# The high part of each weight slab copied in two halves, the first as soon as TensorE is half through the slab two back

## What is computed

```python
def first_block(x, meta_tokens, ...):
    h = rmsnorm(h_res, norm_g[l])
    proj = h @ w_in[l]
    glu_a, glu_b, z_conv, q, f, i, g_rec, m_conv, m_rec = jnp.split(proj, split_idx, axis=-1)
    y_conv = conformer_branch(glu_a, glu_b, z_conv, ...)     # gated conv of width 31, layernorm, silu, @ w_out
    y_rec = hgrn2_branch(q, f, i, g_rec, ...)                # 8 heads, decaying linear recurrence
    merged = jax.nn.sigmoid(m_conv) * y_conv + jax.nn.sigmoid(m_rec) * y_rec
    h_res = h_res + merged @ w_out[l]
def second_block(x, ...):
    n = rms_norm(x, mix_norm_g[l]); proj = jnp.einsum('bsd,de->bse', n, w_in[l])
    mixed = jnp.concatenate([y_a, y_b, y_c], axis=-1)        # chunked attention, short conv, spatial gating
    x = x + jnp.einsum('bse,ed->bsd', mixed, w_out[l])
    hdn = jnp.square(jax.nn.relu(jnp.einsum('bsd,df->bsf', rms_norm(x, mlp_norm_g[l]), w_up[l])))
    x = x + jnp.einsum('bsf,fd->bsd', hdn, w_down[l])
# third block: mLSTM of 4 heads with gates from the projection, pooling over windows of
# 2, 4, 8 and 16 tokens, output projection, layer norm, MLP of 4096, layer norm
```

## Time and profile before

| | us |
|---|---|
| median of 3 runs | 3816.53 |
| lowest and highest | 3816.52, 3818.11 |
| profiled execution, its time | 3818.15 |
| profiled execution, its span | 3816.8 |
| TensorE busy | 3702.0 (97%) |
| VectorE busy | 1701.3 (45%) |
| ScalarE busy | 1177.3 (31%) |
| GpSimd busy | 1095.4 (29%) |
| mean granted clock of TensorE, share of full | 0.986 |

### The profile page before, as it was taken

How to read it: one execution, slowest core, us unless ns; L and a number is a source line. 1 busy time by engine, 2 the same in 40 slices (tenths; PEclk the granted TensorE clock), 3 DMA queues, 4 the chain that set the end, 5 groups by cost and what they waited for, 6 DMA issues and landing times.

```text
span 3816.8 us, 42159 instructions
## 1 busy us (share of the span) xinstructions
PE 3702.0 (97%) x17644; PEld 3027.0 (79%) x17644; DVE 1701.3 (45%) x2132; ACT 1177.3 (31%) x1523; POOL 1095.4 (29%) x747
## 2 busy tenths in 40 slices
PE   6999999999999999999999999999999999999998
PEld 6888887888878876777788888887777878888886
DVE  5655624999652473224442222225657652222226
ACT  4554532222241243444321211114323241111113
POOL 3334321222233451111442222224212442222223
PEclk9999999999999999999999999999999999999999
DMA  2000011111232240001221111113111321111112
GB/s 102 28 29 28 28 62 60 56 56 53 69 133 92 97 151 34 33 33 34 100 73 49 45 50 45 50 45 120 49 33 34 105 71 46 50 44 45 50 45 77
DMA packets 64988, 229.29 MB, mean 60 GB/s; under 512 B 7200, under 2 KB 7328, under 8 KB 64672
## 3 DMA queue, kind: packets, MB, share of 16 engines
q1 hardware_dynamic: 64800, 226.60, 18.0%
HBM read 201.40 MB, written 25.17 MB: 59 GB/s over the span
## 4 chain that ended last, share of the span: by engine, by line
PE 88%; DVE 7%; issue 2%; ACT 2%; POOL 1%; DMA 1%; SPq 0%; DVEq 0%; ACTq 0%
PE psum L505 76%; PE psum L617 2%; PE psum L853 2%; PE psum L868 2%; PE psum L883 1%; DVE Ab L2130 1%; PE psum L588 0%; DVE qb L2176 0%; PE psum L702 0%; PE psum L739 0%; POOL wl L3115 0%; PE psum L641 0%; PE psum L640 0%; DVE fb L2095 0%; DVE fb L2087 0%
## 5 line engine op out<-in xcount | busy, mean ns | idle before, releaser
L3115 POOL TENSOR_TENSOR wl<-raw,wh 128x512 fp32r<-128x512 f32 x636 | 889.7, 1419 | 2380.1 <-ACT wh L1185 2380.1
L505 PE MATMUL psum<-hh,wh 128*128 128x512 f32 (+2 forms) x3760 | 1188.4, 392 | 38.2 <-POOL wl L3115 15.7
L505 PE MATMUL psum<-hh,wl 128*128 128x512 f32 (+2 forms) x3760 | 1149.8, 381 | 0.0
L505 PE MATMUL psum<-hl,wh 128*128 128x512 f32 (+2 forms) x3760 | 1145.3, 380 | 0.0
L505 PEld LDWEIGHTS psum<-hh,wh 128*128 128x128 f32 x3760 | 678.4, 191 | 185.6 <-issue 31.2
L505 PEld LDWEIGHTS psum<-hh,wl 128*128 128x128 f32 x3760 | 699.5, 190 | 134.4
L505 PEld LDWEIGHTS psum<-hl,wh 128*128 128x128 f32 x3760 | 698.1, 189 | 133.1
L1185 ACT ACTIVATE wh<-raw 128x1024 fp32r<-128x1024 f32 x318 | 335.0, 1054 | 790.9 <-PE psum L505 784.8
L505 PE MATMUL psum<-hdh,wh 128*128 128x512 f32 x1024 | 334.0, 398 | 5.0 <-DVE B L3016 4.4
L505 PE MATMUL psum<-hdh,wl 128*128 128x512 f32 x1024 | 331.3, 395 | 0.0
L505 PE MATMUL psum<-hdl,wh 128*128 128x512 f32 x1024 | 331.3, 396 | 0.0
(11 more groups left out here) (421 smaller groups left out, 3020.3 us busy)
## 6 DMA issues: line engine op xcount, KB each, us to landing
raw<-in_wts SPq DMA_DIRECT2D x318, 512.0 KB, 3.5
keep_x<-B SPq DMA_DIRECT2D x14, 512.0 KB, 5.8
X<-in_xin SPq DMA_DIRECT2D x8, 520.0 KB, 5.6
keep_sz<-tmp SPq DMA_DIRECT2D x8, 512.0 KB, 2.9
av<-keep_gr SPq DMA_DIRECT2D x8, 512.0 KB, 3.3
tmp<-keep_sz SPq DMA_DIRECT2D x8, 512.0 KB, 3.6
av<-keep_gc SPq DMA_DIRECT2D x8, 512.0 KB, 3.9
xc<-keep_x SPq DMA_DIRECT2D x8, 512.0 KB, 5.8
```

The lines of the kernel that those rows point to most:

```text
L505: ins = pe.matmul(out, w, x[:, k, c0:c0 + width], start=first and n == 0, stop=final and n == 2)
L3115: gp.tensor_tensor(wl[:, s, a], raw[:, s, a], fp(wh[:, s, a]), SUB).then_inc(*c.lo.tick(i, p))
```

## The change

ScalarE copies a slab in two activations of 128x512 instead of one of 128x1024, and each signals for itself: `hi(i, 0)`, `hi(i, 1)`. GpSimd's two halves of wl each wait for their own. The first copy of slab i waits for a new signal of TensorE, `gemm(i - 2, "first")`, given after the k step 3 of slab i - 2 (in `last=True` slabs `h_used(i - 2, 3)`, in down slabs the pass that has that half); the second waits for the end of that slab, as the whole did. A new call `early(n)` stands in ScalarE's list where slabs up to n - 1 and the first half of slab n are to be made. In a few places other steps change their order with it: the rounding of the last tile (`out_high(7, 0)`, `mlp_high(7, 0)`, `last_high(7, 0)`) goes ahead of the last square.

```diff
-    def spent(i):
-        return c.gemm(i, 1 if i in DOWN else 0)
+    def spent(i, p):
+        if i in DOWN:
+            return c.gemm(i, p)
+        if p == 0 and i in BEFORE.values():
+            return c.h_used(i, KT // 2 - 1)
+        return c.gemm(i, 0) if p else c.gemm(i, "first")
...
+                elif k == KT // 2 - 1:
+                    ins.then_inc(*c.gemm.tick(i, "first"))
...
+        def pieces(n):
+            while done[0] < min(n, 2 * NSLAB):
+                i, p = done[0] // 2, done[0] % 2
+                done[0] += 1
+                s, a = i % 2, slice(p * 512, (p + 1) * 512)
+                if p == 0:
+                    se.wait_ge(*c.weight_in[s](i))
+                if i >= 2:
+                    se.wait_ge(*spent(i - 2, p))
+                se.activation(wh[:, s, a], raw[:, s, a], COPY).then_inc(*c.hi.tick(i, p))
...
-                se.activation(wh[:, s, :], raw[:, s, :], COPY).then_inc(*c.hi.tick(i))
+            pieces(2 * n + 2)
+
+        def early(n):
+            pieces(2 * n + 1)
 
         def slab(i):
             split(i + 1)
-            side.turn(KT)
+            side.turn(KT // 2)
+            early(i + 2)
+            side.turn(KT // 2)
...
         for m, tiles in ((5, (0, 1)), (6, (2, 3, 4)), (7, (5, 6))):
             split(OUT2 + m + 5)
             square("n5", m - 1, c.ev_v("x2", m - 1, 1), 1)
+            early(OUT2 + m + 6)
             for k in tiles:
                 mlp_high(k, 0)
-        square("n5", 7, c.ev_v("x2", 7, 1), 1)
         split(MLP2 + 1)
         mlp_high(7, 0)
+        square("n5", 7, c.ev_v("x2", 7, 1), 1)
+        early(MLP2 + 2)
...
             for u, tiles in enumerate(((), (0, 1), (2, 3, 4), (5, 6, 7))):
                 if u:
                     split(base + u + 1)
+                    early(base + u + 2)
                 for k in tiles:
                     high(k, 1)
                 relu_half(base, tmp6, u, 0)
```

More of the change, by code:

```diff
@@ L546, in duo @@
                 ins = three(prs[e], hds[e], i + e, k, k, n == 0, n == KT - 1, hh, hl, META)
-                if n == KT - 1:
+                if n == max(order.index(z) for z in range(KT // 2)):
+                    ins.then_inc(*c.gemm.tick(i + e, "first"))
+                elif n == KT - 1:
                     ins.then_inc(*c.gemm.tick(i + e, 0))
@@ L1193, in duo @@
             for e, n in duo_steps():
+                if n == KT // 2:
+                    early(i + e + 2)
                 if n == KT - 1:
@@ L1201, in last_slab @@
             for k in range(KT - 1):
+                if k == KT // 2:
+                    early(i + 2)
                 side.turn()
@@ L1622, in scalar @@
                 split(SGU + n + 1)
+                early(SGU + n + 2)
             for k in tiles:
@@ L1777, in scalar @@
             i = down_at(MLP2, 7, 0, hf)
-            split(i + 1)
+            if hf == 0:
+                split(i + 1)
+            early(i + 2)
             if hf:
@@ L1808, in scalar @@
                 split(GATES3 + n + 1)
+                early(GATES3 + n + 2)
             for k in tiles:
@@ L1867, in scalar @@
             split(GATES3 + 4 + n + 1)
+            early(GATES3 + 4 + n + 2)
             if n == 1:
@@ L1946, in scalar @@
         rows("m1", R7)
+        early(OUT3 + 4)
         split(OUT3 + 4)
@@ L1982, in scalar @@
         split(i + 2)
+        early(i + 3)
         roots("m2", 0, COPY, scale=1.0 / 256)
@@ L1986, in scalar @@
             half_square("v2", k, 0, c.nrm("m2", k, 0))
+        early(i + 4)
         split(i + 4)
@@ L1990, in scalar @@
             half_square("v2", m, 0, c.ev_v("dn", MLP3, 7, m, 0))
+        early(i + 5)
         split(i + 5)
@@ L1996, in scalar @@
             half_square("v2", k, 1, c.nrm("m2", k, 1))
+        early(i + 6)
         split(i + 6)
@@ L3104, in gpsimd, with pieces, early @@
         done = [0]
-        def split(n):
-            while done[0] <= min(n, NSLAB - 1):
-                i = done[0]
-                done[0] += 1
-                s = i % 2
-                gp.wait_ge(*c.hi(i))
-                for p in range(2):
-                    a = slice(p * 512, (p + 1) * 512)
-                    gp.tensor_tensor(wl[:, s, a], raw[:, s, a], fp(wh[:, s, a]), SUB).then_inc(*c.lo.tick(i, p))
+        def pieces(n):
+            while done[0] < min(n, 2 * NSLAB):
+                i, p = done[0] // 2, done[0] % 2
+                done[0] += 1
+                s, a = i % 2, slice(p * 512, (p + 1) * 512)
+                gp.wait_ge(*c.hi(i, p))
+                gp.tensor_tensor(wl[:, s, a], raw[:, s, a], fp(wh[:, s, a]), SUB).then_inc(*c.lo.tick(i, p))
+        def split(n):
+            pieces(2 * n + 2)
+        def early(n):
+            pieces(2 * n + 1)
         def slab(i):
```

47 lines of the change are left out of this document (33 added, 14 removed).

## The result

| | before | after |
|---|---|---|
| median, us | 3816.53 | 3847.97 |
| lowest and highest | 3815.54, 3818.11 | 3845.35, 3849.36 |
| profiled execution, span | 3816.8 | 3844.0 |
| ratio after / before | | 1.0081, 95% interval 1.0069 to 1.0094 |

**Slower by 31.4 us, 0.8%.** The sign was forecast, the size was half of it (+15), and the time lies outside the range. Both profiled executions are single ones: after's is the fastest of its four runs and before's is 1.6 us above its median, so the two traces differ by 27.2 us and the rest lies between runs.

What follows compares the result with a forecast made beforehand. TensorE, busy for 3702.0 of 3816.8 us, was taken as the bound. 8.7 (heads) + 5.8 (half-width starts) + 1.3 + 0.6 + 0.6 + 0 + 1.0 - 2 - 1 = +15 us, a median of 3831.5 us; range 3808 to 3839.

Steps and rivals of the forecast that it cites:

- The sign: Whole kernel: the change was forecast to make it slower, +15 us, 3831.5 us as a median; slower had chance 0.60.

Runs made afterwards that it cites:

- e8: Kernel before, with GpSimd waiting for VectorE's last product in seven heads and making wl ahead of tile 5's low part at half-width starts: 3805.53 us, ratio 0.997.

## What to carry to other kernels

Before making an operand ready sooner on an engine that shares a port, list which operations of the other engine are less than that much ahead of it, and who waits for them; a helper that starts 0.4 us sooner can cost the critical engine a whole turn. Before placing a step that waits into an in-order queue, ask for each of its waits, not only the obvious one, how late it can be and what stands behind it. And holding an uncritical engine back until the critical operation is done can be worth more than speeding it up: two lines, -19 us, and a third for -23.

## What the runs showed of the hardware

A stall can cost more than it lasts. Seven waits at L617 that shrank by 1.1 us each gave 19.4 us, because behind a wait of 2.82 us TensorE ran at a granted clock of 0.56 to 0.58 for four microseconds, and behind one of 1.74 at 1.00. But no length of wait tells in these traces what follows: behind 3.58 us it was 1.00 once in seven heads of the kernel after, behind 1.75 us it was at the lower level in two of seven heads of e8, and in e8 waits of 0.86 and 0.56 us among small matmuls were followed by 0.65 to 0.67. By the two heads of e8 such a stretch costs 1.5 to 1.6 us and comes or stays away with no edit near it, so a single trace isn't enough to price it.
